# Half states' decay on ScalarE at the end of the heads, and other orders of small operations, in a hybrid attention and state-space decoder layer

## The reference

```
h  = rmsnorm(x) ;  q_a, c_raw, kr_raw, z_attn, z_ssm, xbc, dt = split(h @ w_in)
# attention with a latent cache (8 heads): prompt causal over itself, samples over 2048 cached rows
q = rmsnorm(q_a) @ w_q_b ; q_lat = q_nope @ w_uk ; q_rope, k_rope rotated ; ckv = rmsnorm(c_raw)
o_attn = (softmax(q_lat.ckv + q_rope.k_rope) @ ckv @ w_uv) * silu(z_attn)
# state-space mixer (16 heads of 64, 2 groups, state 128), prompt in chunks of 128:
xs, B, C = silu(causal_conv(xbc)) ; dt = softplus(dt + bias) ; a = -exp(a_log) * dt
y = cb * decay_in @ (xs * dt)  +  C @ states * exp(cumsum a)
# each sampled token: state = exp(a) * state + (xs * dt) B^T ;  y = state C
y_ssm = group_rmsnorm((y + d * xs) * silu(z_ssm))
out = x + rmsnorm(concat(o_attn, y_ssm) @ w_out)
```

## Time and profile before

| | |
|---|---|
| median of 3 runs | 500.34 us (500.3 to 502.52) |
| profiled execution | 500.38 us |
| its span | 498.6 us, mean granted clock 0.997 |
| PE busy | 483.7 us (97%) |
| VectorE busy | 351.4 us (70%) |
| ScalarE busy | 283.0 us (57%) |
| GpSimd busy | 92.6 us (19%) |
| HBM | 209 GB/s over the span |

### The profile page before, as it was taken

One profiled execution on the slowest core, in us unless ns is written; L12 is line 12 of the kernel. 1 busy time (PEld: TensorE's weight loads), 2 busy tenths in 40 slices (PEclk: granted clock), 3 DMA queues, 4 the chain that ended last, 5 costly groups with the idle time before them and its releaser, 6 DMA issues.

```text
span 498.6 us, 12380 instructions
## 1 busy us (share of the span) xinstructions
PE 483.7 (97%) x4756; PEld 423.7 (85%) x4756; DVE 351.4 (70%) x795; ACT 283.0 (57%) x580; POOL 92.6 (19%) x122
## 2 busy tenths in 40 slices
PE   8999999999999999999999998999899999999995
PEld 7999999999999999999999874666566689998883
DVE  4653768693857567555433599698999799998763
ACT  6733412234376474654624995677776869764441
POOL 1641000010000010000000142544555701110500
PEclk9999999999999999999999999999999999999998
DMA  8543222469898989979896331733322676799842
GB/s 284 216 170 122 72 74 96 133 196 359 296 321 285 310 286 306 325 263 326 296 309 219 121 93 53 252 124 115 133 89 95 239 254 208 245 316 388 329 130 84
DMA packets 47852, 106.34 MB, mean 213 GB/s; under 512 B 7881, under 2 KB 13794, under 8 KB 47666
## 3 DMA queue, kind: packets, MB, share of 16 engines
q1 hardware_dynamic: 47650, 105.50, 62.6%
q10 hardware_dynamic: 144, 0.05, 0.1%
HBM read 96.27 MB, written 7.75 MB: 209 GB/s over the span
## 4 chain that ended last, share of the span: by engine, by line
PE 73%; DVE 15%; ACT 5%; issue 3%; POOL 2%; SPq 1%; DMA 1%; DVEq 0%; ACTq 0%; POOLq 0%
PE pm L1794 17%; PE pm L1795 16%; PE pm L1796 16%; PE px L1905 3%; PE px L1930 3%; DVE hring L1430 3%; PE px L2092 2%; DVE u L1180 2%; PE px L1795 1%; PE px L1796 1%; PE px L1794 1%; PE pm L2110 1%; DVE w_lo L1087 1%; POOL hring L1741 1%; PE pm L2080 1%
## 5 line engine op out<-in xcount | busy, mean ns | idle before, releaser
L1794 PE MATMUL pm<-xw_hi,w_lo 128*128 128x260 f32 x520 | 150.5, 289 | 0.0
L1795 PE MATMUL pm<-xw_lo,w_hi 128*128 128x260 f32 x520 | 147.0, 283 | 0.0
L1796 PE MATMUL pm<-xw_hi,w_hi 128*128 128x260 f32 x520 | 146.9, 282 | 0.0
L651 ACT ACTIVATE w_hi<-w_raw 128x1024 fp32r<-128x1024 f32 (+1 forms) x70 | 72.5, 1038 | 81.2 <-PE pm L1796 65.4
L1087 DVE TENSOR_TENSOR w_lo<-w_raw,w_hi 128x1024 fp32r<-128x1024 f32 (+1 forms) x70 | 87.8, 1261 | 31.6 <-ACT w_hi L651 31.5
L1794 PEld LDWEIGHTS pm<-xw_hi,w_lo 128*128 128x128 f32 x520 | 98.0, 188 | 1.6
L1795 PEld LDWEIGHTS pm<-xw_lo,w_hi 128*128 128x128 f32 x520 | 97.9, 188 | 0.1
L1796 PEld LDWEIGHTS pm<-xw_hi,w_hi 128*128 128x128 f32 x520 | 97.9, 188 | 0.0
L1794 PE MATMUL pm<-mix_hi,w_lo 128*128 128x264 f32 x128 | 37.2, 291 | 0.8 <-DVE mixlo_a L1485 0.8
L783 ACT ACTIVATE alpha<-nmh 128x1 f32<-128x1 f32 x16 | 4.7, 295 | 56.1 <-DVE nmh L1193 56.1
L1796 PE MATMUL pm<-mix_hi,w_hi 128*128 128x264 f32 x128 | 36.3, 284 | 0.0
(11 more groups left out here) (315 smaller groups left out, 1098.9 us busy)
## 6 DMA issues: line engine op xcount, KB each, us to landing
page<-in_cache SPq DMA_DIRECT2D x128, 288.0 KB, 4.2
w_raw<-in_w_in SPq DMA_DIRECT2D x32, 512.0 KB, 5.1
w_raw<-in_w_out SPq DMA_DIRECT2D x16, 512.0 KB, 3.9
w_raw<-in_w_tok SPq DMA_DIRECT2D x16, 512.0 KB, 5.8
dec<-ac_dram SPq DMA_DIRECT2D x16, 256.0 KB, 3.6
hring<-in_ssm_state SPq DMA_DIRECT2D x8, 512.0 KB, 6.6
o_ssms<-hring SPq DMA_DIRECT2D x8, 512.0 KB, 6.9
w_raw<-in_w_qb SPq DMA_DIRECT2D x6, 384.0 KB, 2.9
```

What stands on the lines that cost most here:

```text
L651: act.activation(w_hi[s][:, 0:n], w_raw[s][:, 0:n], ACT.Copy).then_inc(a_whi, 1)
L1794: pe.matmul(out, wl, xh, start=start, stop=False)
L1795: pe.matmul(out, wh, xl, start=False, stop=False)
L1796: return pe.matmul(out, wh, xh, start=False, stop=stop)
```

## The change

The decay of halves 0 to 5 is taken from GpSimd and put on ScalarE, at the end of its head: in head 0, after `copy_pt(0, 3)` and `decays(6)`, halves 0 and 1; in heads 1 to 4 half s + 1, ahead of the decay matrices of the next heads. `copy_k(s + 2)` goes ahead of the fourth exponential. At the end of the heads, `gated_square(7)` goes behind the last copies, `mix_high(7)` ahead of `ssm_high(0)`, and on VectorE `mix_low(7)` ahead of `group_scale(2)`. `stack_low(2)` and `(3)` go from the loop of the preparation to behind `head(4)`, `stack_low(7)` from ahead of head 0 into it, behind `head(5)`. On TensorE, `query_lat` goes from step 3 to step 5 of item 18, and the transpose of the samples' B and C goes ahead of `keys(0)`. The updates' waits follow the decays to `a_h`.

```diff
--- before.py
+++ after.py
@@ -323,7 +323,7 @@
     a_vhi, v_vlo = sem("values_hi_done"), sem("values_lo_done")
     a_krh, v_krl, a_qsh, v_qsl = sem("k_rope_hi_done"), sem("k_rope_lo_done"), sem("q_stack_hi_done"), sem("q_stack_lo_done")
     v_scaled, g_scaled, g_fin = sem("out_scaled"), sem("last_out_scaled"), sem("last_out_done")
-    p_tot, g_xe, v_gs, v_sn = sem("group_total"), sem("x_to_end_done_then_state_decayed"), sem("sample_gated"), sem("sample_normed")
+    p_tot, g_xe, v_gs, v_sn = sem("group_total"), sem("x_to_end_done"), sem("sample_gated"), sem("sample_normed")
     g_sqg, v_gm = sem("group_squares_added"), sem("ssm_normed")
     p_x, p_b, p_cb, p_st, p_y = sem("xs_transposed"), sem("b_transposed"), sem("cb_full"), sem("state_full"), sem("y_full")
     p_bct, p_v, p_os, p_ring = sem("bc_transposed"), sem("v_full"), sem("o_sample_full"), sem("ring_full")
@@ -1001,13 +1001,16 @@
                 gated_square(t)
             if s in FALLS:
                 decays(FALLS[s][0][0])
-            exps(s + 1, 3)
             if s + 2 < H:
                 copy_k(s + 2)
+            exps(s + 1, 3)
             copy_pt(s, 2)
             copy_pt(s, 3)
             if s == 0:
                 decays(6)
+                state_decay(0)
+            if s < 5:
+                state_decay(s + 1)
             if s == 5:
                 gated_square(6)
                 hi(NIN)
@@ -1020,12 +1023,12 @@
         hi(NIN + 1)
         copy_pt(H - 1, 0)
         copy_pt(H - 1, 1)
-        gated_square(7)
         mix_high(H - 2)
         copy_pt(H - 1, 2)
         copy_pt(H - 1, 3)
+        gated_square(7)
+        mix_high(H - 1)
         ssm_high(0)
-        mix_high(H - 1)
         ssm_high(1)
         hi(NIN + 2)
         ssm_high(2)
@@ -1422,10 +1425,7 @@
             if n == 0:
                 dve.wait_ge(v_dx, 1)
             dve.wait_ge(s_bcs[b % 2], 16 * (b // 2 + 1))
-            if n < 6:
-                dve.wait_ge(g_xe, 2 * NCH + 4 * n + 4)
-            else:
-                dve.wait_ge(a_h, 4 * (n - 6) + 4)
+            dve.wait_ge(a_h, 4 * n + 4)
             for t in range(4 * g, 4 * g + 4):
                 dve.scalar_tensor_tensor(hring[b][:, t, :], bcs[b % 2][:, g, :], dxs[:, 0, t, b:b + 1], hring[b][:, t, :], ALU.mult, ALU.add).then_inc(v_h, 1)
 
@@ -1521,13 +1521,11 @@
                 sample_out(1)
             if n >= 5:
                 head(n - 5)
-            if n in (6, 7):
-                stack_low(n - 4)
         state(2 * NCH - 1)
         for h in range(3, 5):
             head(h)
-        stack_low(4)
-        stack_low(5)
+        for h in range(2, 6):
+            stack_low(h)
         dve.wait_ge(p_os, 1)
         dve.tensor_tensor(z[:, 0:H, NT:TT], z[:, 0:H, NT:TT],
                           px[:, 3, 0:2 * P].rearrange("p (h b k) -> p h b k", h=H, k=4)[:, :, :, 0], ALU.mult).then_inc(v_os, 1)
@@ -1544,7 +1542,6 @@
                 inverse_sum(0, b - 1)
         inverse_sum(0, 3)
         y_pair(0)
-        stack_low(7)
 
         for s in range(H - 1):
             mask_max(s + 1, 0)
@@ -1571,6 +1568,7 @@
                 dve.wait_ge(a_zh, 1)
                 dve.tensor_tensor(mixlo_a[:, 0:H, NT:TT], zs, mix_hi[:, 0:H, NT:TT].bitcast(F), ALU.subtract)
                 head(5)
+                stack_low(7)
             for h in MASKS[1].get(s, ()):
                 head(h)
             inverse_sum(s + 1, 3)
@@ -1587,8 +1585,8 @@
         lo(NIN + 1)
         mix_low(H - 2)
         gated(H - 1)
+        mix_low(H - 1)
         group_scale(2)
-        mix_low(H - 1)
         group_scale(3)
         ssm_low(0)
         ssm_low(1)
@@ -1731,18 +1729,8 @@
             pool.tensor_tensor(total, sq[SQ0[3] % 2][:, 0:NT] if t % 4 == 1 else total, sq[(SQ0[3] + t) % 2][:, 0:NT], ALU.add)\
                 .then_inc(g_sqg, 1)
 
-        def state_decay(n):
-
-            b = n // 2
-            if n == 0:
-                pool.wait_ge(a_dx, 1)
-            pool.wait_ge(s_x[b], 32)
-            for t in range(4 * (n % 2), 4 * (n % 2) + 4):
-                pool.tensor_scalar(hring[b][:, t, :], hring[b][:, t, :], dxs[:, 1, t, b:b + 1], 0.0, ALU.mult, ALU.add).then_inc(g_xe, 1)
-
         for b in range(4):
             norm(0, b)
-        state_decay(0)
         for s in range(H - 1):
             if s == 6:
                 pool.wait_ge(v_dot, 24)
@@ -1755,8 +1743,6 @@
                 add_square(t)
             norm(s + 1, 2)
             norm(s + 1, 3)
-            if s < 5:
-                state_decay(s + 1)
         add_square(7)
 
         def out_add(j):
@@ -1818,7 +1804,7 @@
                         norm_total(0)
                     if (i, r, k) == (13, 2, 0):
                         dt_totals()
-                    if (i, r, k) == (18, 0, 3):
+                    if (i, r, k) == (18, 0, 5):
                         query_lat()
                     if 8 * r + k in place:
                         n_ = place[8 * r + k]
@@ -2156,12 +2142,12 @@
                 xs_t(n + 2)
             if n == 3:
                 cb_products()
+        pe.wait_ge(a_cvs, 2)
+        pe.wait_ge(v_cb, 2)
+        pe.transpose(px[0:32, 3, 0:P], cvs[:, 1, 8:12, :], cm[:, M_ID, :]).then_inc(p_bct, 1)
         pe.wait_ge(v_xdt, 2 * NCH)
         keys(0)
         state(2 * NCH - 1)
-        pe.wait_ge(a_cvs, 2)
-        pe.wait_ge(v_cb, 2)
-        pe.transpose(px[0:32, 3, 0:P], cvs[:, 1, 8:12, :], cm[:, M_ID, :]).then_inc(p_bct, 1)
         pe.wait_ge(a_bct, 1)
         for g in range(2):
             for r in range(2):
```

## The result

The changed kernel takes 509.48 us (median of 4 runs, 508.2 to 511.08), the kernel before in the same comparison 500.32 us. The ratio on record is 1.0175, interval [1.0134, 1.0216]: slower, by 1.3 to 2.2%. The profiled execution took 508.20 us, span 506.4, and is compared here with the 500.38 of before: +7.82. It is the fastest of the four.

A forecast was written before the change was run, and what follows sets the result against it. The prediction took TensorE, 73% of the span, as the bound. Its terms -0.7 +2.7 +2.4 -0.8 +3.4 +0.6 -0.6 -0.5 sum to +6.5 on 500.38 us, so 506.9 us, range 503.3 to 510.

The forecast's parts named there:

- step 1: query_lat two steps later on TensorE: fills its wait for the last rotated query, -0.7 us.
- 2, stack order: Before the heads: later stack_low(2) and (3) hold stack_high(7), delaying TensorE's sample-head products by +2.7 us.
- step 3: TensorE's clock falls in the 4.4 us gap before the sample-head products; some 5 us at half pace, +2.4 us.
- step 5: Half states' decay on ScalarE: VectorE's first update waits, delaying head 1's fourth score block +3.4 us; later heads' load +0.6.
- step 6: Key copies ahead of the fourth exponential: only the copy's own time is won, in head 2, -0.6 us.
- step 7: New order at the end of the heads: TensorE's 0.8 us wait for a low half shrinks, -0.5 us.
- step 4: stack_low(7) behind head(5): no longer ahead of head 1's first mask_max on VectorE, -0.8 us.
- case (c): Clock also falls in the second gap, at head 1's fourth score block: 2 to 2.4 us more, 509.1; chance 0.2.
- (d): One of the two delays, 3.4 or 2.7 us, is hidden and its clock cost halved: 502 to 503; chance 0.06.
- (e): Relief of VectorE decides and TensorE loses no time in the heads: -4.6 us, 495.8; chance 0.05.

The follow-up runs named there:

- run 1: Changed kernel with stack_low(2), stack_low(3) and the B/C transpose back where they were: 503.66 us, ratio 1.0056 to the kernel before.
- run 12: Kernel before with only the new stack_low(2) and (3) order and the moved B/C transpose: 506.03 us, ratio 1.0097.
- Runs 8: Kernel before with only the decays of halves 0 to 5 on ScalarE, half 0 ahead of the fourth exponential: 502.15 us, ratio 1.002.
- run 9: Kernel before with only the key copies moved ahead of the fourth exponential, decays staying on GpSimd: 501.39 us, ratio 1.001.
- runs 10: Kernel before with decays on ScalarE (half 0 ahead of the key copies) and key copies ahead of the fourth exponentials: 500.42 us, ratio 0.9984.
- Run 5: Kernel before with only the new order at the end of the heads: 502.07 us, ratio 1.0011.
- Runs 7: As run 4, but with the old order at the end of the heads: 499.51 us, ratio 0.996 to the kernel before.
- run 4: Changed kernel with the old stack order and half 0's decay ahead of the key copies in head 0: 499.18 us, ratio 0.997 to the kernel before.
- run 2: Changed kernel with the decays of halves 0 to 5 back on GpSimd: 505.77 us, ratio 1.0095 to the kernel before.
- run 11: As run 4, with the first eight cache page loads ahead of a weight load on SyncE's queue: 499.9 us, ratio 0.9977 to the kernel before.
- run 3: Changed kernel with 14 and 12 unread matmuls ahead of TensorE's two long waits: 505.14 us, ratio 1.0095 to the kernel before.

## Why the prediction was right, and where a size was off

It said 506.9 us in a range of 503.3 to 510.0; 509.48 came. Direction, both long waits and their causes were right, and the sum fell short by 1.3 us in the profiled run (+6.5 against +7.8). That it came so near is partly luck. Measured less forecast, by the milestones, steps 1 and 2 are off by +0.8, step 3 by -1.0, the second fall that was not in the sum by +1.7, steps 5 and 6 in the later heads by -1.35, step 7 by +1.2; step 4 and the wait in step 5 by 0.1 each. By its steps:

**1, query (-0.7):** won at the first page (-0.57 from +0.13), then mostly lost again by the second, which had not landed. In run 1, where the stack order is undone, the difference to before is +0.18 at the query and -0.08 at the sample-head products, so 0.26 is left. The sentence "what follows on TensorE has no wait of this size" looked at waits that were there, not at one that would come.

**2, stack order (+2.7):** in run 12 the products start 2.86 us later than before (3.16, less the 0.30 that it was late at the first page already). In the changed kernel steps 1 and 2 together were to be +2.0 and were +2.8, most of the difference being step 1's. The starts, stack_low from 308.45 and stack_high(7) at 309.9, were 308.56 and 310.00.

**3, first clock fall (+2.4):** it fell; the price was 1.39 in the changed kernel and 2.65 in run 12. The 5 us at half pace, taken from the program's start, were 3.4 and 6.8 in the falls measured. Part of each passed before TensorE resumed; it worked at half clock for 3.0 and 5.6 us, and half of that, 1.5 and 2.8, is near the 1.39 and 2.65 lost. The start was also a weak source: its matmuls take twice as long, but the granted clock of the kernel before shows no fall there (same columns):

```profile
5.00:7.00 2.00, 2.00 (x8) 1.73 (x8) 1.09 (x3) 1.21 (x3) 0.00 (x0) 1.00 1.00 339
```

**4, stack_low(7) (-0.8):** -0.91.

**5, decay on ScalarE:** the first delay was +3.4 and came as +3.48; VectorE's wait of 3.4 was 3.37. The load was to cost 0.6 and step 6 to win as much, nothing together. They won 1.35 from 349 to 394. Runs 8, 9 and 10 show the term that failed: "this relief is inside the +0.6". The prediction had the relief itself right, 1.0 us in three waits of VectorE for GpSimd's decays, and also that the gates and sums go on blocking VectorE. What it missed is that VectorE's waits set the length of these heads once the key copy is out of the way, so that they come off TensorE's time (10.53 us in place of 10.98), while ScalarE at 10.22 of 10.53 just fits.

**6, key copies (-0.6):** alone they win nothing (run 9), with the decays on ScalarE they make the difference between +1.0 and -0.6. In head 2 of run 9 TensorE no longer waits 1.85 us for the key copy but 1.50 for the probabilities, which is the limit that the step named (outs(h, 2) needs copy_pt(h, 2)). A gain for one part alone was the wrong question.

**7, end of the heads (-0.5):** +0.70. Run 5 shows the wait traded for one on mixlo_s. Of the rest, 0.48 lies ahead of the output stage. Runs 7 and 10, with the old end, also give back 0.5 from the last heads to the end (-1.05 to -0.59 and -0.57 to -0.02), and both wait for the last head's probabilities, which the kernel before does not. The changed kernel does so too:

```profile
401.23 0.92 PE L2096 MATMUL pm<-pt,v 128*128 128x256 f32 x4 [0.65 <-ACT pt L941]
```

**The second fall** was case (c), given 0.2, at 2 to 2.4 us. It came, at 1.67. It was judged the less likely although the gap of 3.4 us stood well above the 2.7 that had been read from the end of the program; nothing in the profile spoke for one fall and against the other. Run 1's profile has the same gap and no fall, and the mean clocks of its other executions fit a fall in three of five, so two cases with chances were the right form; that the chance should have been higher is argued from these few and not shown.

The trace now bears on the Trainium skill (TensorE: Matmul & The Clock Gate, Part 1) as well: gaps of the same 3.3 us with a fall and without one agree with its statement that the phase is not tied to the program, though two profiles do not show it.

Cases (d) and (e) did not come. The time (e) hoped for needs both delays gone: run 4, where they are, won 1.5 us by the medians and not 4.6. Of the difference, 1.5 us is the wait for probabilities that has taken the place of the 1.85.

## What to carry to other kernels

When an operation moves to an engine with an in-order queue, its place there matters more than its length: 1.3 us of decay left a wait of 0.3 us ahead of the key copies, and of 3.3 us, with a clock fall behind it, after them. Two edits of one loop can each be worth nothing or less and together be a gain, when each alone leaves the limit that the other removes; try them as a pair. When an overlap seems to go, look at the next operation too: here it only moved from one to the other. Price a stall of TensorE as the stall and a possible fall of the clock behind it, and take the price of the fall as a range.

## What the runs showed of the hardware

TensorE's granted clock fell to half after waits of 4.56 us (three profiles: the changed kernel, runs 2 and 12), 3.33 (the changed kernel) and 1.90 (run 11), and not after one of 3.32 (run 1). The fall began between 1.3 us before TensorE resumed (run 12) and 0.8 us after (run 11). It lasted 3.4 us in four cases and 6.8 in run 12, though TensorE worked without a gap once it had resumed. It cost 1.39 and 1.67 us in the changed kernel, 1.63 in run 2 and 2.65 in run 12, close to half of the time that TensorE worked at half clock. Fourteen and twelve small matmuls that nothing reads, ahead of the two waits, kept the clock at 1.00 and won 4.3 us (run 3).

Four VectorE scalar_tensor_tensor operations on 128x128 floats take 1.14 us beside an idle GpSimd, 2.28 beside one of its tensor_tensor operations of 1.3 us and 3.44 beside two: VectorE stands nearly as long as these run (up to 1.37 us for one operation with a median of 0.35). The first operation of dots(n) is held in the same way, 1.38 us in place of 0.29 (runs 10 and 9). Moving the decay from GpSimd to ScalarE did not take such an overlap away; it moved one from the update to the dots.
